# Attention heads of a two-layer diffusion backbone: one row of query blocks, context block third, next head's keys ahead of a weighted job

## What is computed

```python
qn, qr = _mla_q(h, ...)                  # 8 heads, 128 + 64 rotated columns
kvu = (ckv @ w_ukv).reshape(B, Lk, 8, 128 + 128)
k_nope, v = kvu[..., :128], kvu[..., 128:]
s = einsum('bqhd,bkhd->bhqk', qn_b, k_nope) + einsum('bqhr,bkr->bhqk', qr_b, k_rope)
p = softmax(s * ATTN_SCALE)
o = einsum('bhqk,bkhd->bqhd', p, v)      # by blocks of 128 queries
return o.reshape(B, Lq, 8 * 128) @ w_o
```

## Time and profile before

| | |
|---|---|
| median of 3 runs | 3497.03 us (3493.97 to 3501.98) |
| the profiled execution's own time | 3493.42 us |
| its span, first to last instruction | 3491.9 us |
| mean granted clock of TensorE | 0.963 of full |
| PE busy | 93% |
| DVE busy | 51% |
| ACT busy | 28% |
| POOL busy | 5% |

### The profile page before, as it was taken

How to read it: one execution, slowest core, us unless ns; L and a number is a source line. 1 busy time by engine, 2 the same in 40 slices (tenths; PEclk the granted TensorE clock), 3 DMA queues, 4 the chain that set the end, 5 groups by cost and what they waited for, 6 DMA issues and landing times.

```text
span 3491.9 us, 48286 instructions
## 1 busy us (share of the span) xinstructions
PE 3260.1 (93%) x18847; PEld 3150.7 (90%) x18847; DVE 1783.6 (51%) x2985; ACT 961.7 (28%) x1324; POOL 163.2 (5%) x201
## 2 busy tenths in 40 slices
PE   7999999998999999998879799989879999999997
PEld 4999999997999999998879687878769999999996
DVE  8766888786333333334635556555654333333333
ACT  4333111124111111112322545463633111111114
POOL 3000000002000000002201000000000000000002
PEclk8999999999999999999889999999989999999998
DMA  6444433321111111111113101010001111111111
GB/s 213 143 149 139 129 93 117 104 79 31 43 42 42 42 42 42 42 42 40 43 40 138 41 9 39 13 34 27 13 13 31 43 42 42 42 42 42 42 42 61
DMA packets 272682, 210.39 MB, mean 60 GB/s; under 512 B 15102, under 2 KB 243756, under 8 KB 272572
## 3 DMA queue, kind: packets, MB, share of 16 engines
q1 hardware_dynamic: 260908, 163.50, 15.4%
q0 software_dynamic: 11664, 45.39, 3.7%
HBM read 185.10 MB, written 23.76 MB: 60 GB/s over the span
## 4 chain that ended last, share of the span: by engine, by line
PE 76%; DVE 13%; issue 4%; ACT 3%; DMA 2%; SPq 0%; POOL 0%; DVEq 0%; ACTq 0%; POOLq 0%
PE set L548 62%; PE set L1040 4%; PE set L1028 3%; DVE pa L2021 2%; PE turned L791 2%; DVE soft L2383 1%; PE set L625 1%; DVE tmp L1838 1%; DMA tmp<-in_ada_w 1%; ACT pr L1103 1%; DVE hlo L1847 1%; DVE ptl L2399 1%; DVE pah L1962 1%; DVE x L1815 1%; PE set L582 1%
## 5 line engine op out<-in xcount | busy, mean ns | idle before, releaser
L548 PE MATMUL set<-hhi,whi 128*128 128x384 f32 x2856 | 656.6, 337 | 6.8 <-DVE wlo L1732 4.7
L548 PE MATMUL set<-hlo,whi 128*128 128x384 f32 x2856 | 652.1, 336 | 0.0
L548 PE MATMUL set<-hhi,wlo 128*128 128x384 f32 x2856 | 651.2, 335 | 0.0
L2039 DVE SCALAR_TENSOR_TENSOR x<-set,mod,x 128x128 f32<-128x128 f32 x744 | 412.9, 612 | 289.3 <-PE set L548 289.3
L548 PEld LDWEIGHTS set<-hhi,whi 128*128 128x128 f32 x2856 | 509.3, 189 | 7.7 <-issue 5.3
L548 PEld LDWEIGHTS set<-hlo,whi 128*128 128x128 f32 x2856 | 512.3, 189 | 0.0
L548 PEld LDWEIGHTS set<-hhi,wlo 128*128 128x128 f32 x2856 | 511.8, 189 | 0.0
L1732 DVE TENSOR_TENSOR wlo<-wraw,whi 128x1024 fp32r<-128x1024 f32 x207 | 252.2, 1220 | 466.7 <-ACT whi L1103 437.6
L1103 ACT ACTIVATE whi<-wraw 128x1024 fp32r<-128x1024 f32 x207 | 217.4, 1052 | 702.9 <-PE set L548 700.5
L1103 ACT ACTIVATE tmp<-set 128x1152 f32<-128x1152 f32 x97 | 110.1, 1135 | 706.5 <-PE set L548 696.8
L548 PE MATMUL set<-ghi,whi 128*128 128x384 f32 x1296 | 295.3, 335 | 3.6 <-DVE x L2039 3.5
(11 more groups left out here) (237 smaller groups left out, 4167.4 us busy)
## 6 DMA issues: line engine op xcount, KB each, us to landing
wraw<-in_f_w_in SPq DMA_DIRECT2D x176, 256.0 KB, 3.0
adu<-in_ada_w SPq DMA_DIRECT2D x48, 512.0 KB, 6.0
wraw<-in_f_w_out SPq DMA_DIRECT2D x88, 256.0 KB, 2.8
wraw<-in_a_w_in SPq DMA_DIRECT2D x64, 256.0 KB, 3.2
v_scratch<-vst POOLq DMA_DIRECT2D x16, 576.0 KB, 3.0
vld<-v_scratch POOLq DMA_DIRECT2D x16, 576.0 KB, 4.3
q_scratch<-tmp POOLq DMA_DIRECT2D x16, 576.0 KB, 3.4
aldr<-in_ada_w SPq DMA_DIRECT2D x8, 1024.0 KB, 11.6
```

Source lines behind the costliest of these rows:

```text
L548: last = nc.tensor.matmul(ps[:, b, 0:cols], w, m[:, b * cols:(b + 1) * cols], start=(i == 0 and p == 0), stop=(i == n - 1 and p == 2))
L2039: last = v.scalar_tensor_tensor(dst, src, k.mod[:, gate + n, c:c + 1], dst, ALU.mult, ALU.add)
```

## The change

The heads are no longer closed one by one. All 8 heads make one row of blocks, and the code is written as a prologue, a loop of three turns, and a last part:

- **Order.** The blocks of a head are taken as 1, 2, 0, 3 to 8 (`ORDER`). The context block is the third (`CTX_AT`). Its scores stand in one job with the last weighted product of the head before; its own weighted product stands in the job of block 5's place (`head_job(5, 2, None, h, None)`).
- **Next head's first scores.** The first two score jobs of the next head stand in the end of this head, with the last turns of this head inside them.
- **Queries by thirds.** The parts of the next head's queries are made in three pieces of 384 columns, one after round 1, one after round 4, one after block 8, each when those columns are no longer read. ACT has 6 instructions for a head where there were 4, and DVE 6 where there were 4.
- **Keys.** Every head, not the first of a pair only in another place, has the keys of the next head made after its last score job, ahead of the turns of block 6 and of the third weighted product. ACT and DVE take their parts in that order too: queries' last third, keys, then the turns of block 6.
- **Weights of keys and values.** Both units, of 512 columns each, go into the two halves of slot 1 (`kv_split`); `w_o` goes into slot 0 (`o_split`). For the next pair `kv_split` stands on ACT and DVE after rounds 2 and 3 of head 1. The first `o_split` stands at the end of head 1, the second between the output jobs. In the last head two whole `split` stand in the places of `kv_split`.
- **Pair's output.** The values' two jobs and the output's eight stand after the next head has begun, as values, four output jobs, values, four output jobs.
- **Normalise.** Near the end of a head `normalise` of the next head's first block stands ahead of `turned(8, True)` on ACT.

Jobs of a pair go from 34 to 32. The core of the diff (PE's order, and ACT's and DVE's where they differ from it):

```diff
+KV_SLOT, OUT_SLOT = 1, 0
+ORDER, CTX_AT = (1, 2, 0, 3, 4, 5, 6, 7, 8), 2
...
+    def head_job(self, s, off, late, h=None, pair=None):      # PE
+        ps = self.open()
+        last = self.scores(ps, ORDER[s], late, off)
+        if h is not None:
+            self.probs_turned()
+            last = self.weighted(ps, h, pair)
+        self.close(last)
+    def head_first(self, h, before):
+        self.head_job(2, 0, None, 1 - h if before else None, 3)
+        self.turn_probs(0, False, 1)
+        self.B.step()
+    def head_middle(self, h):
+        self.head_job(3, 0, 0)
+        self.turn_probs(1, False, 1)
+        self.head_job(4, 1, 1, h, 0)
+        self.turn_probs(2, False, 2)
+        self.head_job(5, 2, None, h, None)
+        self.turn_probs(3, False, 3)
+        self.head_job(6, 3, 3)
+        self.turn_probs(4, False, 4)
+        self.head_job(7, 4, 4, h, 1)
+        self.turn_probs(5, False, 5)
+        self.head_job(8, 5, 5)
+        self.B.step(5)
+    def head_rest(self, h):
+        self.head_middle(h)
+        if h == 1:
+            self.unit_ready()
+        self.keys_job(1 - h)
+        self.turn_probs(6, False, 1)
+        self.turn_probs(6, True, 1)
+        self.weighted_job(h, 2)
+        self.turn_probs(7, False, 2)
+        self.next_head_ready()
+        self.head_job(0, 2, 7)
+        self.turn_probs(8, False, 3)
+        self.head_job(1, 3, 8)
+        self.B.step(3)
+    def last_head(self):
+        self.head_middle(1)
+        self.turn_probs(6, False, 1)
+        self.turn_probs(6, True, 1)
+        self.weighted_job(1, 2)
+        self.turn_probs(7, False, 2)
+        self.turn_probs(7, True, 2)
+        self.turn_probs(8, False, 3)
+        self.turn_probs(8, True, 3)
+        self.weighted_job(1, 3)
...
+        self.head_job(0, 0, None)                             # PE, heads()
+        self.head_job(1, 0, None)
+        self.head_first(0, False)
+        with repeat(pe, HEADS // 2 - 1, ...):
+            self.head_rest(0)
+            self.head_first(1, True)
+            self.head_rest(1)
+            self.head_first(0, True)
+            self.O.step(10)
+            self.unit_ready(1)
+            self.values_job(range(0, 6))
+            pe.wait_ge(k.o_ready, self.O.at())
+            self.pair_out(2)
+            self.values_job(range(6, 11))
+            self.pair_out(3)
+            self.U.step(4)
+        self.head_rest(0)
+        self.head_first(1, True)
+        self.last_head()
...
+    def kv_split(self, half):                                 # ACT; DVE alike
+        self.act(k.whi[:, KV_SLOT, half * 512:half * 512 + 512], k.wraw[:, s, 0:512]).then_inc(k.hi_done, 1)
+    def head_round(self, h, s, pair=-1):                      # ACT
+        if pair != -1:
+            self.eng.wait_ge(self.k.mm_done, self.J.at(1))
+        self.turned(s, False)
+        self.exponentials(s + 2, 3)
+        if pair != -1:
+            self.read_out(h, pair)
+        self.turned(s, True)
+        self.normalise(s + 2, 3)
+        self.B.step()
+    def head_middle(self, h, ahead):                          # ACT; DVE has queries_lo
+        self.head_round(h, 1)
+        if ahead:
+            self.queries_hi(0)
+        self.head_round(h, 2, 0)
+        if h == 1:
+            self.kv_split(0) if ahead else self.split()
+        self.head_round(h, 3, None)
+        if h == 1:
+            self.kv_split(1) if ahead else self.split()
+        self.head_round(h, 4)
+        if ahead:
+            self.queries_hi(1)
+        self.head_round(h, 5, 1)
+        self.exponentials(8, 3)
+    def head_rest(self, h):                                   # ACT
+        self.head_middle(h, True)
+        self.queries_hi(2)
+        self.keys_hi()
+        self.turned(6, False)
+        self.turned(6, True)
+        self.normalise(8, 3)
+        self.B.step()
+        self.weighted_read(h, 2)
+        self.turned(7, False)
+        self.turned(7, True)
+        self.turned(8, False)
+        self.exponentials(0, 3)
+        self.normalise(0, 3)
+        self.B.step()
+        self.turned(8, True)
+        self.exponentials(1, 3)
+        self.normalise(1, 3)
+        self.B.step()
+        if h == 1:
+            self.o_split()
+    def head_rest(self, h):                                   # DVE
+        self.head_middle(h, True)
+        self.queries_lo(2)
+        self.keys_lo()
+        self.turned(6, False)
+        self.turned(6, True)
+        self.B.step()
+        self.weighted_read(h, 2)
+        self.turned(7, False)
+        self.turned(7, True)
+        self.maxima(0, 3, 0)
+        self.turned(8, False)
+        self.inverse_sum(3)
+        self.B.step()
+        self.turned(8, True)
+        self.maxima(1, 3, 0)
+        self.inverse_sum(3)
+        self.B.step()
+        if h == 1:
+            self.o_split()
```

More of the change, by code:

```diff
@@ L1025, in scores @@
             if p == 3 and between is not None:
[L1026 removed]
+                self.turn_probs(between, True, off)
             for bank, lo, n in chunks:
@@ L1056, in head_pair, with heads @@
+    def heads(self):
         k, pe = self.k, self.eng
-        ku, vu = self.U.odd(), self.U.odd(1)
+        assert self.U.odd() == KV_SLOT
         self.unit_ready()
[L1059 to L1095, removed]
@@ new lines, in last_head, with values_hi @@
+    def last_head(self):
+        self.head_middle(1, False)
+        self.turned(6, False)
+        self.turned(6, True)
+        self.normalise(8, 3)
+        self.weighted_read(1, 2)
+        for s in (7, 8):
+            self.turned(s, False)
+            self.turned(s, True)
+        self.weighted_read(1, 3)
+    def values_hi(self, lo, n):
+        self.eng.wait_ge(self.k.mm_done, self.J.at(1))
+        self.kv_hi(v_parts(self.k.vh, self.k.sets[self.J.odd()], lo, n))
+        self.J.step()
@@ new lines, in heads @@
+    def heads(self):
+        k, a, J = self.k, self.eng, self.J
+        for b in range(BANKS):
+            self.queries_hi(b)
+        self.keys_hi()
+        self.values_hi(0, 6)
+        self.values_hi(6, 5)
+        for s in range(2):
+            self.exponentials(s, s + 1)
+            self.normalise(s, s + 1)
+        self.head_first(0, False)
+        self.turned(0, True)
+        self.normalise(2, 3)
+        self.B.step()
+        with repeat(a, HEADS // 2 - 1, (J, 32), (self.U, 4), (self.T, 50), (self.G, 2),
+                    (self.B, 18), (self.O, 10), (self.F, 8)):
+            self.head_rest(0)
+            self.head_first(1, True)
+            self.turned(0, True)
+            self.normalise(2, 3)
+            self.B.step()
+            self.head_rest(1)
+            self.head_first(0, True)
+            self.normalise(2, 3)
+            self.values_hi(0, 6)
+            J.step(4)
+            self.o_split()
+            self.values_hi(6, 5)
+            J.step(4)
+            self.turned(0, True)
+            self.B.step()
+        self.head_rest(0)
+        self.head_first(1, True)
+        self.turned(0, True)
+        self.normalise(2, 3)
+        self.B.step()
+        self.last_head()
@@ L2291, in queries @@
         J.step(2)
-        self.split()
+        if last:
+            self.kv_split(0)
+            self.kv_split(1)
+        else:
+            self.split()
         for h in range(2):
```

363 lines of the change are left out of this document (221 added, 142 removed).

## The result

The changed kernel takes 3483.67 us (median of 5 runs, 3476.76 to 3489.05) against 3496.7 us for the kernel before beside it: a ratio of 0.9961 with a 95% interval of 0.9944 to 0.9978. I had forecast 3501. Run again later it came to 3477.88 us and 0.995 (0.9937 to 0.9964).

What follows compares the result with a forecast made beforehand. PE was taken to bound the kernel, through idle time and low clock. Lost time +3, late turns +2, clock -1 and thirds 0.3 gave +4 to +5 us: 3501 us on the median's scale, 8-in-10 range 3483 to 3518.

Steps and rivals of the forecast that it cites:

- The lost time of the changed kernel: PE's lost time over the heads after the change: about 86 us, with 19.3 for a pair in the loop.
- The clock: PE's time lost at 1.2 GHz in the heads: 29 us after the change against 30 before, 1 less.
- Keys' stretch: Low clock in the keys' stretch of seven heads, slowing the product behind: 2.3 us each (1.4 to 2.7), 16 in all.
- kv_split's stretch: Low clock in head 1's context stretch, its slowness partly hidden under the wait for DVE: 6 us for four.
- The late turns: Late turns inside score jobs, seven a head against five before: 0.1 to 0.15 us more each, 16 times, 2 us.
- The lost time before: PE's lost time in the four pairs before the change: 66.6 us idle and 16 hidden, about 83 us.
- The sum without the clock: Whole change apart from clock: +3 us lost time, +2 for late turns, 0.3 for the thirds at the start.
- The thirds: Next head's queries made in three pieces: some tenths of a microsecond more a head, all but the last third hidden.
- A: Slower rival: clock stays low over head 1's second split wait, next product also slow; about 3515 us, chance 0.24.
- B: Faster rival: fewer clock falls, 16 us instead of 29, and DVE's queue in head 1 cheaper; 3480 us, chance 0.21.
- C: Faster rival: the keys' job covers the chain, block 6's turns free at once; 32 us less, 3469 us, chance 0.06.
- The signs I had named: Profile signs: `ptl` waits of 3 to 3.5 us behind keys, two split waits, loop turn 165 to 168 us, idle and clock limits.

Runs made afterwards that it cites:

- fill_after: Changed kernel with extra unused matmuls in PE's waits in each head's keys' stretch and the last head's end: 3463.76 us, 0.9909 of the kernel before.
- fill_before: Kernel before the change with extra unused matmuls in PE's waits at the ends of the heads: 3469.05 us, 0.992 of the kernel before.
- queries_last: Changed kernel with all three thirds of the next queries behind block 8, ahead of the keys' parts: 3498.0 us, 1.001 of the kernel before.
- turns_ahead: Changed kernel with block 6's turns ahead of the keys on ACT and DVE, and PE's third group inside the keys' job: 3435.45 us, 0.982 of the kernel before.

## Why the prediction was wrong, step by step

**The lost time of the changed kernel was right.** A turn of the loop was to lose 19.3 us; it has 16.7 idle and 12 waits that hide 0.2 each: 19.1. The places are those forecast: behind every keys' job 3.04 to 3.37 and 0.93 to 1.02 (forecast 3.4 and 1.15), 2.93 and 1.71 at the splits (2.9 and 1.9), 0.77 to 0.88 ahead of the late turn in head 0 (0.8), 0.96 to 1.05 ahead of the fourth product (1.0). Less was lost at the prologue's start, 1.18 and 0.82 against 3.2, and at the whole splits of the last head, 3.92 and 1.23 against 6.7.

**The clock was the step that failed.** I held it at "29: 1 less" than the 30 before. Before, it was 28.3. After, it was 17.7 to 19.4. From one weighted product to the next, the changed kernel and fill_after differ by 12.6 us over the seven intervals that begin with the product behind the keys, by 5.0 from the last but one product to the end, and by 1.8 everywhere else. Against my terms:

- Keys' stretch: 2.3 a head forecast, 16 in all; measured 1.8 a head (12.6 / 7), below the middle of my bounds of 1.4 and 2.7.
- kv_split's stretch: 6 forecast; nothing that the runs show. In the three turns of the loop the clock did not fall there at all; in fill_after it did, and it cost nothing, as PE waits for DVE in that place. I wrote that its slowness would be "partly" hidden. It was hidden wholly.
- Last head's end: 6 forecast, 5.0 measured.
- Prologue: 1 forecast; no run of the changed kernel fills it, and by its first round (5.93 us against 4.64 in fill_before) it is at most 1.3.

I charged low clock for stretches where PE is not the one that comes last. A slow engine costs only where something waits for it.

**The late turns were the second, by 2 us.** I charged 0.1 to 0.15 for each break of a round. In the changed kernel eleven rounds take 4.00 to 4.02 us from one group of eight turns to the next, each with a late turn in its midst (such as 2162.81 to 2166.83). That is 0.79 for the eight turns, 0.22 for the late two, and the 3.00 that 15 score matmuls take where nothing breaks them (from 2127.18 on). So the break has no price. I had worked it out from the 4.18 of the earlier trace rows, a stretch that ends in a weighted product; such stretches take 4.11 to 4.18 in the changed kernel too, and 4.16 to 4.25 before.

**The lost time before was put too low.** From group to group no full round of the kernel before is below 4.34 us. The rows of one of them say why:

```profile
2191.97 1.03 PE L791 MATMUL turned<-ident,pr 128*128 128x128 f32 x8
...
2192.51 1.48 DVE L2383 TENSOR_REDUCE soft<-set 128x1 f32<-128x1280 f32 x1
...
2194.12 1.29 DVE L2399 TENSOR_TENSOR ptl<-turned,pth 128x512 fp32r<-128x512 f32 x2
...
2194.87 0.44 PE L791 MATMUL turned<-ident,pr 128*128 128x128 f32 x2
```

The late turn comes 2.90 us after its group, 0.75 behind the start of `ptl`, which stands behind a maximum. In the changed kernel's round of 2162.81 no maximum is in front of `ptl`, and the late turn comes after 2.62 us, 1.03 behind the start of `ptl`: it was not held up. All 24 such rounds of the kernel before wait in this way, for 0.3 to 0.6 us, and in 8 of them the wait is too short to be marked as idle. Counted from start to start of PE's matmuls, an estimate from the two traces, the lost time of the stage is 86 us before and 87 after, where I had 83 and 86.

**The sum without the clock** was to be +5.3 us (3 lost, 2 late turns, 0.3 thirds); the filled kernels show -4.1. Of these 9.4 us, 3.6 are the wait for ACT's exponential that full clock uncovers in the kernel before, 2 the late turns, and about 2.7 the lost time. About 1 us stays open.

**The thirds:** their price of some tenths is borne out by the pieces' durations, but I left out that their places carry the change. I took the keys' stretch with one third ahead of the keys (4.55 a head lost, 5.5 if that third were late too) and never asked what it would be with all three there. queries_last shows it: 2.1 a head more, past my bound.

**The rivals.** A did not come. In fill_after the clock falls at the place and behind the wait named, for 3.4 us, and costs nothing. In the loop of neither the changed kernel nor fill_after does it stay low over the second wait and the product, so the dear half of A is not tested. A's 3515 was also on the profile's scale; on the median's, 17 above 3501 is 3518. B names the right cause, the clock won back, and gave 3480 for it; but its other half, a shorter queue of DVE in head 1, did not happen: the waits are there in full. C is refuted by the rows, 3.18 behind each keys' job; turns_ahead shows what it would have been worth. C had this at 32 us, from 3.4 us and "half of those falls"; built, it brought 49 to 51, of which 45 in the seven heads.

**Luck.** The first median, 3483.67, lies 0.7 us above the lower end of my range; the repeat, 3477.88, lies below it. The forecast of 3501 had the wrong direction, and that the range held once is luck.

**The signs I had named** were of mixed worth. The waits came as written, the loop's turn was 160.0 and not 165 to 168, and the limits that were to tell B and A (idle under 13 or over 21, mean clock over 0.96 in the heads) were not reached: 16.7, and 0.95 in the stage, though 0.97 in a turn of the loop. Yet it was B's mechanism: a gain of 9 us moved the stage's mean clock only from 0.94 to 0.95, too little for the limit that I had set.

## What to carry to other kernels

Price a low clock only in stretches where the slow engine is the last to arrive; where it waits for another anyway, slow work fills the wait. Extra matmuls in PE's waits, in both kernels, are a cheap way to measure what the clock costs; look also for waits that only the filled kernel has, since slow work covered them. Compare rounds that begin and end in the same kind of work. Look for waits that come from the written order of two in-order queues: three moves of a few lines each, found in the changed kernel's waits, were worth five to six times the change itself.

## What the hardware showed that I had not expected

- More work made both kernels faster: 240 more matmuls in the heads of the kernel before (3562 to 3802), 28.3 us less; 159 more in the changed one, 17.7 to 19.4 less.
- The same wait of PE, 2.93 and 2.94 us at the same place of the code, let the granted clock fall to 1.2 GHz in one kernel and not in the other. The Trainium skill (TensorE: Matmul & The Clock Gate, HAM oscillation) has waits between bursts throttle the clock. The traces agree that falls come behind waits, and show that a single wait's length does not decide it.
- The heads' start lies between 1926.5 and 1941.4 us in kernels whose code ahead of it is nearly the same. A difference of two single spans below some 15 us says nothing here; the stage's length, 649.8 and 648.1 us in two profiles of one kernel, tells more.
